# The triangular inverse of the delta-rule layer spread over two tile steps

## The chip, the cores and the metric

The kernel runs on one core of one Trainium2 chip, as one launch. The metric is the device time of that launch in microseconds (us); lower is better. The engines are PE (TensorE, matmuls; its weight loads are shown as PEld), DVE (VectorE), ACT (ScalarE), POOL (GpSimd) and SP (SyncE, which issues the DMAs here). Each engine works through its own list of instructions in order, and waits on semaphores for the others.

## What is computed

One layer of an encoder with two mixers. The change touches one stage of it, the chunked gated delta rule (DeltaNet): 4 heads of 128, 1024 prompt tokens with a state that starts at zero, and 64 sample tokens with a given state.

```python
def chunk_gated_delta(q, k, v, g, beta, s0):
    ...
    A = jnp.where(strict, jnp.einsum('bhnid,bhnjd->bhnij', k_beta, k) * dmask, 0.0)
    eye = jnp.eye(C, dtype=F32)
    T = lax.linalg.triangular_solve(eye + A, jnp.broadcast_to(eye, A.shape),
                                    left_side=True, lower=True)
    u = T @ v_beta
    w = T @ (k_beta * jnp.exp(decay)[..., None])
    qk = jnp.einsum('bhnid,bhnjd->bhnij', q, k) * dmask
    ...
    def step(S, inp):
        u_n, w_n, qk_n, qd_n, kd_n, gl_n = inp
        v_new = u_n - w_n @ S
        o_n = qd_n @ S + qk_n @ v_new
        S = S * gl_n[..., None, None] + jnp.einsum('bhck,bhcv->bhkv', kd_n, v_new)
        return S, o_n
```

## The kernel before

The whole layer is one hand-ordered program: for every engine there is a function that writes its instructions in the order in which they run, and semaphores (`g_X`, `g_Pb` and so on) hold the engines together. Before the delta-rule stage come the input projection, the S5 mixer and a gated unit (GLU); behind it come the output projection (`wo_pe`) and the feed-forward part, in which PE is busy nearly all the time.

The stage works on `TILES` = 9 tiles of 128 tokens: 8 of the prompt (`PTILES`) and one with the 64 sample tokens. One tile step `t` does the following for the four heads.

- **Preparation of a tile** (called n): `turn_kq` transposes k and q on PE, ACT sums their squares (`squares_k`, `squares_q`), POOL makes scales of them (`scales`), `gram` gives k times k, `coupling` on DVE makes A of it, `turn_A` transposes A, ACT copies it out (`keep_A`), and DVE builds the first blocks of the inverse and the masked levels of A (`first_blocks`, `first_level`, `later_levels`). `turn_v` transposes v into the bank in which k stood, once ACT has taken k from it (`k_decayed`); `scores`, `causal` and `q_decayed` prepare q's part.
- **The inverse**: blocks double in six levels. In a level PE makes P from X and the level's part of A (`level`, first half, L1128; 8 matmuls of 64x64), ACT copies P out of PSUM (`keep_P`, L1282), PE makes two products of P and X (L1137, L1139; 16 matmuls), DVE adds them to X (`grow_X`, L1507). Each next level needs that sum. Level 5 (L1125, L1133) is half as large. An f32 matmul leaves two records in the trace, so the counts there are twice these. The sample tile has five levels.
- **The state** (`state`): k times the state S (L1150), DVE makes the right sides (`right_sides`, L1514), new values V (L1154), ACT copies them (`keep_V`, L1302), then per head two matmuls of the output and one of the new state (L1161 to L1163), and DVE updates S (`new_state`, L1522).
- **The output** of tile t - 1 is scaled (POOL `out_scale`, DVE `out_rows`), transposed (`turn_o`, L1192) and written (`mix`), and two pieces of unrelated work stand in every step: `ada_rows` (L1170) and `ada_columns` (L1186), with `mod_rows` and `mod_columns` on DVE.

The order is that of the code: in step t PE runs levels 0 to 5 of tile t, and between them the preparation of tile t + 1. A level on PE waits for ACT (`g_Pb`) and DVE (`g_X`) per head; each head has a PSUM bank of its own for all levels. Banks 4 to 7 are for outputs, k and v, q and scores, and A. Two sets of most buffers alternate. In the last step ACT and DVE also split the first output weights into two parts (`wo_high`, L1695, and `wo_low`, L1699), with `tile_hi` and `tile_lo` for the first tiles of the mix. `wo_pe` waits for the last state (`g_S`).

## Time and profile before

| | |
|---|---|
| median of 3 runs | 1418.52 us (1415.66 to 1419.41) |
| the profiled execution's own time | 1418.34 us |
| its span, first to last instruction | 1416.6 us |
| PE busy, share of the span | 1365.3 us, 96% |
| delta-rule stage, from the first matmul of an inverse to the first of the output projection | 394.92 to 592.01 us |
| mean granted TensorE clock | 0.989 |

Times inside the trace count from the start of the span. 1.7 us lie around the span. A row of the timeline gives start, length, engine, line, operation, output and inputs and a count of merged records; a bracket behind it says how long the engine was idle before and who ended that.

### The profile page before, as it was taken

What the parts mean: (1) busy time and instruction counts of PE and PEld (TensorE: products, weight loads), DVE (VectorE), ACT (ScalarE), POOL (GpSimd) and SP (SyncE); (2) the same over time, 40 slices, a digit from 0 to 9 for tenths busy, and PEclk for the clock granted to TensorE, in tenths of its full rate; (3) what the DMA queues carried; (4) which work ended last, traced back from release to release, by engine and by line L of the source; (5) the groups of instructions that cost most, each with busy time, mean ns of one, the idle gap of its engine ahead of it and who ended that gap; (6) DMA issues with size and microseconds to landing.
All of it is one profiled execution on the core that took longest, in us unless ns stands there. A gap on an engine that the chain in (4) does not pass through costs nothing.

```text
span 1416.6 us, 29230 instructions
## 1 busy us (share of the span) xinstructions
PE 1365.3 (96%) x10652; PEld 1243.7 (88%) x10652; DVE 948.4 (67%) x1593; ACT 590.8 (42%) x1455; POOL 569.3 (40%) x645
## 2 busy tenths in 40 slices
PE   6999899989989999999999999999999999999997
PEld 4899899988978888888799999999999997887675
DVE  6517786774366666788879656666666567576388
ACT  6524344345566656525544333333333325443220
POOL 4887857771033434233331443432443434000051
PEclk8999999999999999999999999999999999999999
DMA  9431435335364545432133454554444448997794
GB/s 345 124 107 42 113 101 134 104 88 152 98 217 132 164 134 166 139 124 75 67 105 105 135 175 145 163 187 159 131 152 157 149 154 331 357 373 255 266 326 173
DMA packets 184409, 234.64 MB, mean 166 GB/s; under 512 B 17708, under 2 KB 118640, under 8 KB 184304
## 3 DMA queue, kind: packets, MB, share of 16 engines
q1 hardware_dynamic: 180128, 221.36, 48.3%
q10 hardware_dynamic: 4176, 11.89, 2.1%
q8 instruction: 65, 1.06, 0.3%
q14 instruction: 40, 0.33, 0.1%
HBM read 170.29 MB, written 61.73 MB: 164 GB/s over the span
## 4 chain that ended last, share of the span: by engine, by line
PE 61%; DVE 7%; ACT 4%; issue 3%; POOL 1%; DMA 1%; SPq 0%; POOLq 0%; DVEq 0%; ACTq 0%
PE bank L2350 30%; PE bank L2264 11%; PE bank L305 3%; PE bank L1674 2%; PE bank L1128 2%; PE bank L1137 2%; PE bank L1634 2%; PE bank L2281 1%; PE bank L1139 1%; PE bank L1170 1%; ACT hp L1724 1%; PE bank L1161 1%; DVE stat L1757 1%; ACT vp L1275 1%; DVE xt L1792 1%
## 5 line engine op out<-in xcount | busy, mean ns | idle before, releaser
L2264 PE MATMUL bank<-split 128*128 128x512 f32 x924 | 212.3, 390 | 3.0 <-DVE split L2397 2.3
L2264 PEld LDWEIGHTS bank<-split 128*128 128x128 f32 x924 | 172.7, 188 | 44.8 <-DVE split L2393 5.2
L2350 PE MATMUL bank<-Tlo,rh 128*128 128x272 f32 x640 | 184.7, 289 | 0.0
L2350 PE MATMUL bank<-Thi,rh 128*128 128x272 f32 x640 | 184.2, 288 | 0.0
L2350 PE MATMUL bank<-Thi,rl 128*128 128x272 f32 x640 | 184.0, 288 | 0.0
L305 PE MATMUL bank<-hT_hi,whi 128*128 128x384 f32 (+1 forms) x504 | 166.7, 331 | 2.4 <-DVE wlo L295 2.2
L305 PE MATMUL bank<-hT_hi,wlo 128*128 128x384 f32 (+1 forms) x504 | 164.9, 327 | 0.0
L305 PE MATMUL bank<-hT_lo,whi 128*128 128x384 f32 (+1 forms) x504 | 164.8, 327 | 0.0
L2350 PE MATMUL bank<-hT_lo,rh 128*128 128x272 f32 x480 | 138.5, 289 | 0.0
L2350 PE MATMUL bank<-hT_hi,rl 128*128 128x272 f32 x480 | 138.4, 288 | 0.0
L2350 PE MATMUL bank<-hT_hi,rh 128*128 128x272 f32 x480 | 137.9, 287 | 0.0
L2350 PEld LDWEIGHTS bank<-Thi,rl 128*128 128x128 f32 x640 | 120.5, 188 | 0.0
L2350 PEld LDWEIGHTS bank<-Thi,rh 128*128 128x128 f32 x640 | 120.5, 188 | 0.0
L2350 PEld LDWEIGHTS bank<-Tlo,rh 128*128 128x128 f32 x640 | 120.4, 188 | 0.0
L1963 DVE TENSOR_TENSOR rl<-sums,rh 128x512 fp32r<-128x512 f32 x80 | 61.7, 773 | 85.6 <-ACT rh L1959 85.0
L2368 ACT ACTIVATE split<-rW 128x512 fp32r<-128x512 f32 x77 | 48.6, 631 | 138.4 <-PE bank L2264 57.5
L2393 DVE TENSOR_TENSOR split<-rW,split 128x512 fp32r<-128x512 f32 x77 | 56.6, 738 | 67.7 <-ACT split L2368 67.4
L305 PEld LDWEIGHTS bank<-hT_hi,whi 128*128 128x128 f32 x504 | 95.1, 189 | 4.0 <-DVE wlo L295 2.5
L1959 ACT ACTIVATE rh<-sums 128x512 fp32r<-128x512 f32 x80 | 49.1, 625 | 111.0 <-PE bank L2350 71.1
L305 PEld LDWEIGHTS bank<-hT_lo,whi 128*128 128x128 f32 x504 | 95.1, 189 | 0.0
L305 PEld LDWEIGHTS bank<-hT_hi,wlo 128*128 128x128 f32 x504 | 95.0, 189 | 0.0
L2350 PEld LDWEIGHTS bank<-hT_hi,rh 128*128 128x128 f32 x480 | 90.7, 189 | 0.0
(450 smaller groups left out, 3358.3 us busy)
## 6 DMA issues: line engine op xcount, KB each, us to landing
wada<-w_ada SPq DMA_DIRECT2D x12, 2048.0 KB, 9.1
raw<-w_up SPq DMA_DIRECT2D x40, 512.0 KB, 5.0
wsum<-w_down SPq DMA_DIRECT2D x11, 1024.0 KB, 5.6
wt<-wsum SPq DMA_DIRECT2D x11, 1024.0 KB, 4.0
rW<-wt SPq DMA_DIRECT2D x44, 256.0 KB, 6.6
split<-split SPq DMA_DIRECT2D x22, 512.0 KB, 5.2
wraw<-w_in SPq DMA_DIRECT2D x21, 512.0 KB, 4.4
rows<-convrow ACTq DMA_DIRECT2D x16, 577.5 KB, 3.7
```

Of the source, the lines that this page charges most:

```text
L305: last = nc.tensor.matmul(ps[banks[c]][:, 0:cw], w[:, slot, k * P:(k + 1) * P], a[:, k, c0:c0 + cw], start=(k == 0 and n == 0), stop=(k == ...
L1128: last = pe.matmul(ps[h][q, 0:HB], Lc[x][q, l, h, :], Xc[x][q, h, 0, :], start=True, stop=True)
L1137: pe.matmul(ps[h][q, P:P + HB], Xc[x][q, h, 1, :], Pb[q, h, 0:HB], start=True, stop=True)
L1139: last = pe.matmul(ps[h][q, P + HB:2 * P], Pb[q, h, 0:HB], Xc[x][q, h, 1, :], start=True, stop=True)
L1634: last = pe.matmul(ps[up_bank(1, j, c)][:, 0:cw], w[:, j, k * P:(k + 1) * P], a[:, k, c0:c0 + cw], start=(k == 0 and n == 0), stop=(k == K ...
L1674: last = pe.matmul(ps[2 * s + h][0:n, :], a[:, s, k * P:k * P + n], w[:, k, cols], start=(k == 0 and m == 0), stop=(k == KD - 1 and m == 2))
L1959: act.activation(ring_hi[slot4(m, n)], operand(i, n, m), ACT.Copy).then_inc(on["st_hi"], 1)
L1963: dve.tensor_tensor(ring_lo[slot4(m, n)], operand(i, n, m), ring_hi[slot4(m, n)].bitcast(F32), ALU.subtract).then_inc(on["st_lo"], 1)
L2264: last = pe.matmul(ps[down_bank(q, r)][:], a[:, rows], w, start=(k == 0 and m == 0), stop=(k == KH - 1 and m == 2))
L2350: last = pe.matmul(ps[banks[c]][:, 0:NC], w[:, ks], a, start=(n < 3 and k == 0 and p == 0), stop=(k == 3 and p == 2), skip_group_check=True)
L2368: act.activation(w_hi_of(s), raw_w(s), ACT.Copy).then_inc(on["d_hi"], 1)
L2393: dve.tensor_tensor(w_lo_of(s), raw_w(s), w_hi_of(s).bitcast(F32), ALU.subtract).then_inc(on["d_lo"], 1)
```

## The change

- **The inverse over two steps.** Step t now has three rounds (`round_of`). Round r does level 3 + r of tile t and level r of tile t + 1: P of the one, P of the other, then the products of the one and of the other. Before the loop stand levels 0 to 2 of tile 0 alone, with the preparation of tile 1 between them.
- **Preparation two tiles ahead** (n = t + 2, `AHEAD_OF`), all of it behind the rounds. It needs a third set of `stg`, `kdec` and `sc` and a second `Pb`; the load of q, k, v is issued for tile t + 3.
- **Pairs of heads.** Two heads share a PSUM bank for P and the products: even tiles have banks 0 and 1, odd tiles 2 and 3. ACT copies P, and DVE adds, for two heads at once (2 instructions for 4, twice as wide), and V likewise; semaphores count pairs.
- **State part split** into `read_state`, `new_values` and `outputs`, with `turn_q`, `turn_o`, `turn_v` and `ada_columns` between them; `turn_A`, `scores` and `ada_rows` follow all four heads' outputs. `read_state` waits until the next tile's level 2 has left its bank.
- **Smaller scale formulas.** q's scale isn't applied before the norm of the output any more; POOL does 9 small operations per tile where it did 12 (the two of 8 columns become 4 wide), `scales_k` waits for k's squares alone, and `causal` stands ahead of `q_decayed`, which now waits for the outputs of step t (`g_kv`), since it fills a buffer that they read.
- **End of the stage.** Four pairs of `wo_high` and `wo_low` move from the last step into the one before it. Step 7 has no preparation, and the last step has two levels left.

```diff
-        (kdec0, QK0, qd0, vp0, Pb, Rb, Vb, ob, junk, Sst, Xc0, Xf0), endD = seq(
-            WO2, ("kdec0", hp), ("QK0", hp), ("qd0", hp), ("vp0", hp), ("Pb", hp), ("Rb", hp), ("Vb", hp), ("ob", hp),
+        (kdec2, QK0, qd0, vp0, vp1, Pb0, Rb, Vb, ob, junk, Sst, Xc0, Xf0), endD = seq(
+            WO2, ("kdec2", hp), ("QK0", hp), ("qd0", hp), ("vp0", hp), ("vp1", hp), ("Pb0", hp), ("Rb", hp), ("Vb", hp), ("ob", hp),
...
+        stg, Pb = (stg0, stg1, stg2), (Pb0, Pb1)
+        Lc, kdec, QK, qd, vp, Xc, Xf = (Lc0, Lc1), (kdec0, kdec1, kdec2), (QK0, QK1), (qd0, qd1), (vp0, vp1), (Xc0, Xc1), (Xf0, Xf1)
...
-        lv = lambda t, l, h: (t * LV + l) * HEADS + h
+        PAIRS = HEADS // 2
...
+        ROUNDS = LV // 2
+        AHEAD_OF = 2
...
+                    sp.wait_ge(on["g_E"], (t + 2) * 3 + 3)
+                    decay_rows(t + 4)
+                if t + 3 < TILES:
+                    sp.wait_ge(on["g_kS"], (t + 1) * HEADS)
+                    sp.wait_ge(on["g_qd"], t + 1)
+                    qkv(t + 3)
                 if 1 <= t and t + 1 < TILES:
...
-                for h in range(HEADS):
+                if l in (0, ROUNDS):
+                    pe.wait_ge(on["g_S"], count(t if l else t - 1) * HEADS)
+                for p in range(PAIRS):
...
+            def level_X(t, l):
+
+                x = t % 2
+                for p in range(PAIRS):
+                    pe.wait_ge(on["g_Pb"], lvp(t, l, p) + 1)
+                    for i, h in enumerate((2 * p, 2 * p + 1)):
+                        if l == LV - 1:
...
+            def round_of(t, r):
+
+                units = [(u, l) for u, l in ((t, ROUNDS + r), (t + 1, r)) if 0 <= u < TILES and l <= top(u)]
+                for u, l in units:
+                    level_P(u, l)
+                for u, l in units:
+                    level_X(u, l)
+
+            def read_state(t):
+                if t + 1 < TILES:
+                    pe.wait_ge(on["g_X"], lvp(t + 1, ROUNDS - 1, PAIRS - 1) + 1)
...
-                    pe.matmul(hb(h, 0), stg[:, x, k_ + h, :], Sst[:, st, h, :], start=True, stop=True).then_inc(on["g_kS"], 1)
+                    if t:
+                        pe.wait_ge(on["g_S"], (t - 1) * HEADS + h + 1)
+                    pe.matmul(kS_of(h), stg[t % 3][:, k_ + h, :], Sst[:, state_of(t), h, :], start=True, stop=True).then_inc(on["g_kS"], 1)
+
+            def new_values(t):
                 pe.wait_ge(on["g_Xf"], since("g_Xf", t + 1))
+                pe.wait_ge(on["g_R"], t * HEADS + HEADS)
                 for h in range(HEADS):
-                    pe.wait_ge(on["g_R"], t * HEADS + h + 1)
-                    pe.matmul(hb(h, 3), Xf[x][:, h, :], Rb[:, h, :], start=True, stop=True).then_inc(on["g_V"], 1)
+                    pe.wait_ge(on["g_X"], lvp(t, top(t), h // 2) + 1)
...
+            def outputs(t, heads):
+                x, st = t % 2, state_of(t)
                 pe.wait_ge(on["g_qd"], t + 1)
                 pe.wait_ge(on["g_QK"], t + 1)
...
+            level_P(0, 0)
+            turn_k(1)
+            level_X(0, 0)
+            level_P(0, 1)
+            gram(1, 0)
+            gram(1, 1)
+            level_X(0, 1)
+            level_P(0, 2)
+            turn_q(1, ALL)
+            level_X(0, 2)
+            turn_v(1, ALL)
+            turn_A(1)
+            scores(1)
             for t in range(TILES):
-                n, more = t + 1, t + 1 < TILES
-                level(t, 0)
+                n = t + AHEAD_OF
+                more = n < TILES
+                for r in range(ROUNDS):
+                    round_of(t, r)
                 if more:
-                    turn_kq(n)
-                level(t, 1)
-                level(t, 2)
+                    turn_k(n)
+                    gram(n, 0)
+                    gram(n, 1)
+                read_state(t)
+                if more:
+                    turn_q(n, ALL)
                 if t:
                     turn_o(t - 1)
-                level(t, 3)
                 if more:
-                    scores(n)
-                level(t, 4)
-                if more:
-                    gram(n)
+                    turn_v(n, ALL)
+                new_values(t)
                 if t:
                     ada_columns(t - 1)
+                outputs(t, ALL)
                 if more:
-                    level(t, 5)
                     turn_A(n)
-                    turn_v(n)
-                state(t)
+                    scores(n)
                 if t < PTILES:
                     ada_rows(t)
...
             def keep_P(t, l):
                 rows = DOWN if l == LV - 1 else slice(0, P)
-                for h in range(HEADS):
-                    act.wait_ge(on["g_P"], lv(t, l, h) + 1)
-                    act.activation(Pb[rows, h, 0:HB], ps[h][rows, 0:HB], ACT.Copy).then_inc(on["g_Pb"], 1)
+                for p in range(PAIRS):
+                    act.wait_ge(on["g_P"], lvp(t, l, p) + 1)
+                    act.activation(Pb[t % 2][rows, pair(p), 0:HB], bank_of(t, p)[rows, 0:P].rearrange("p (h c) -> p h c", c=HB),
+                                   ACT.Copy).then_inc(on["g_Pb"], 1)
 
...
-                n, more = t + 1, t + 1 < TILES
-                if more:
-                    keep_P(t, 0)
-                    keep_P(t, 1)
-                    squares_k(n)
-                    keep_P(t, 2)
-                    squares_q(n)
+                n = t + AHEAD_OF
+                more = n < TILES
+                if t < PTILES:
                     keep_P(t, 3)
-                    decay(n)
+                    keep_P(t + 1, 0)
+                    if more:
+                        decay_diff(n, FIRST2)
                     keep_P(t, 4)
-                    decay_exp(n)
-                    k_decayed(n)
+                    keep_P(t + 1, 1)
+                    if more:
+                        decay_diff(n, LAST2)
                     keep_P(t, 5)
+                    keep_P(t + 1, 2)
                     whole_X(t)
-                    keep_A(n)
-                    v_scaled(n)
+                    if more:
+                        decay_exp(n)
+                        decay_row(n)
+                        squares_k(n)
+                        k_decayed(n)
+                        squares_q(n)
                     keep_V(t)
+                    if more:
+                        v_scaled(n)
+                        keep_A(n)
+                    else:
+                        act.wait_ge(on["g_X0"], 2 * TILES)
+                        act.wait_ge(on["g_QK"], TILES)
+                        act.wait_ge(on["g_qd"], TILES)
+                        wo_high(act, 0)
+                        wo_high(act, 1)
                     squares_o(t)
+                    if not more:
+                        wo_high(act, 2)
...
             def q_decayed(n):
+                pool.wait_ge(on["g_E"], n * 3 + 3)
+                pool.wait_ge(on["g_kv"], count(n - 1) * HEADS)
+                pool.tensor_tensor(qd[n % 2][:], stg[n % 3][:, q_:q_ + HEADS, :], erow[:], ALU.mult).then_inc(on["g_qd"], 1)
+
...
-                if t:
-                    out_scale(t - 1)
-                if t + 1 < TILES:
-                    scales(t + 1)
-                    q_decayed(t + 1)
-                    causal(t + 1)
-            out_scale(TILES - 1)
+                n = t + AHEAD_OF
+                if n < TILES:
+                    scales_k(n)
+                    scales_q(n)
+                    causal(n)
+                    q_decayed(n)
...
+                    if l == LV - 1:
...
-                        dve.tensor_copy(Xf[x][UP, h, DOWN], ps[h][UP, P + HB:2 * P]).then_inc(on["g_X"], 1)
...
-                n, more = t + 1, t + 1 < TILES
+                n = t + AHEAD_OF
+                more, nxt = n < TILES, t + 1 < TILES
                 if t:
                     mod_rows(t - 1)
-                grow_X(t, 0)
-                if not more:
-                    wo_low(dve, 0)
-                grow_X(t, 1)
+                for r in range(ROUNDS):
+                    if ROUNDS + r <= top(t):
+                        grow_X(t, ROUNDS + r)
+                    if nxt:
+                        grow_X(t + 1, r)
+                        if r == 0:
+                            keep_scores(t + 1)
                 if t:
                     out_rows(t - 1)
-                if not more:
...
-                    wo_low(dve, 2)
-                grow_X(t, 3)
+                right_sides(t)
...
-                if not more:
-                    wo_low(dve, 3)
-                grow_X(t, 4)
...
                     coupling(n)
-                if more:
-                    grow_X(t, 5)
...
+                elif nxt:
+                    wo_low(dve, 0)
+                    wo_low(dve, 1)
                 else:
+                    wo_low(dve, 4)
                     tile_lo(dve, 0, 0)
                 new_state(t)
                 if more:
-                    keep_scores(n)
+                    first_level(n)
```

PE in step 1 before: level 0, and the transposes of the next tile behind it (Xc is X, Lc the level's part of A).

```order
L1128 MATMUL bank<-Xc_136,Lc_138 64x64 x8
L1137 MATMUL bank<-Pb,Xc_136 64x64 x2
L1139 MATMUL bank<-Xc_136,Pb 64x64 x2
L1137 MATMUL bank<-Pb,Xc_136 64x64 x2
L1139 MATMUL bank<-Xc_136,Pb 64x64 x2
L1137 MATMUL bank<-Pb,Xc_136 64x64 x2
L1139 MATMUL bank<-Xc_136,Pb 64x64 x2
L1137 MATMUL bank<-Pb,Xc_136 64x64 x2
L1139 MATMUL bank<-Xc_136,Pb 64x64 x2
L1078 MATMUL bank<-ident,stg 128x128 x4
L1082 MATMUL bank<-ident,stg 128x128 x4
```

PE in step 0 after, from the start of the first round.

```order
L1161 MATMUL bank<-Xc_153,Lc_119 64x64 x8
L1161 MATMUL bank<-Xc_139,Lc_141 64x64 x8
L1175 MATMUL bank<-Pb_147,Xc_153 64x64 x2
L1177 MATMUL bank<-Xc_153,Pb_147 64x64 x2
L1175 MATMUL bank<-Pb_147,Xc_153 64x64 x2
L1177 MATMUL bank<-Xc_153,Pb_147 64x64 x2
L1175 MATMUL bank<-Pb_147,Xc_153 64x64 x2
L1177 MATMUL bank<-Xc_153,Pb_147 64x64 x2
L1175 MATMUL bank<-Pb_147,Xc_153 64x64 x2
L1177 MATMUL bank<-Xc_153,Pb_147 64x64 x2
L1175 MATMUL bank<-Pb_156,Xc_139 64x64 x2
```

Where one P was followed by its own products, P of a second tile stands between them, and after four heads' products (8 rows) come the other tile's instead of transposes.

PE before, from the gram matrix to the first head's outputs.

```order
L1186 MATMUL bank<-sel,modrow_123 128x2 x4
L1125 MATMUL bank<-Xc_136,Lc_138 64x64 x4
L1133 MATMUL bank<-Xc_136,Pb 64x64 x4
L1101 MATMUL bank<-ident,Am 128x128 x4
L1107 MATMUL bank<-ident,stg 128x128 x4
L1150 MATMUL bank<-Sst,stg 128x128 x4
L1154 MATMUL bank<-Rb,Xf_137 128x128 x4
L1161 MATMUL bank<-Sst,qd_134 128x128
L1162 MATMUL bank<-Vb,QK_133 128x128
L1163 MATMUL bank<-Vb,kdec_132 128x128
```

PE after, from the end of the rounds to the outputs.

```order
L1104 MATMUL bank<-ident,stg_155 128x128 x4
L1125 MATMUL bank<-stg_155 128x128 x4
L1199 MATMUL bank<-Sst,stg_116 128x128 x4
L1110 MATMUL bank<-ident,stg_155 128x128 x4
L1138 MATMUL bank<-ident,stg_155 128x128 x4
L1206 MATMUL bank<-Rb,Xf_154 128x128 x4
L1216 MATMUL bank<-Sst,qd_144 128x128
L1217 MATMUL bank<-Vb,QK_143 128x128
L1218 MATMUL bank<-Vb,kdec_133 128x128
L1216 MATMUL bank<-Sst,qd_144 128x128
L1217 MATMUL bank<-Vb,QK_143 128x128
```

The level between them is gone, `turn_A` has left the stretch, and k, gram, q and v of a tile two ahead stand around the read of the state.

POOL at the start of the stage, before.

```order
L1383 TENSOR_TENSOR sc<-sc 128x4
L1393 TENSOR_TENSOR EB<-E,triu 128x512
L1388 TENSOR_TENSOR qd_142<-stg,erow 128x512
L1410 MEMSET Sst 128x512
L1413 MEMSET Xf_151 64x4x64
L1413 MEMSET Xf_137 64x4x64
L1377 TENSOR_SCALAR sc<-sc 128x8
```

POOL there after; the rows after the gap are those of tile 1.

```order
L1489 TENSOR_SCALAR sc<-sc 128x4
L1499 TENSOR_TENSOR EB<-E,triu 128x512
L1494 TENSOR_TENSOR qd_144<-stg_116,erow 128x512
L1513 MEMSET Sst 128x512
L1516 MEMSET Xf_154 64x4x64
L1516 MEMSET Xf_140 64x4x64
...
L1489 TENSOR_SCALAR sc<-sc 128x4
L1499 TENSOR_TENSOR EB<-E,triu 128x512
L1494 TENSOR_TENSOR qd_138<-stg_117,erow 128x512
```

Ahead of EB now stands q's one operation; EB comes ahead of qd for the later tiles as well, and tile 1 has its EB and qd before the loop.

## Rows read from the trace of the kernel before

**Rows 1.** The page, part 1: busy time, share of the span and instructions.

```profile
PE 1365.3 (96%) x10652; PEld 1243.7 (88%) x10652; DVE 948.4 (67%) x1593; ACT 590.8 (42%) x1455; POOL 569.3 (40%) x645
```

**Rows 2.** Busy time by stretch: steps 1, 2 and 8; us, then each engine, clock, DMA.

```profile
417.10:439.50 22.40, 22.19 (x360) 18.95 (x356) 14.91 (x49) 13.88 (x71) 7.92 (x15) 1.00 0.50 154
439.50:462.10 22.60, 22.39 (x360) 19.01 (x356) 14.96 (x49) 13.92 (x71) 8.00 (x15) 1.00 0.49 153
...
575.00:592.00 17.00, 15.27 (x281) 13.97 (x278) 15.93 (x42) 13.11 (x39) 3.12 (x5) 1.00 0.41 141
```

**Rows 3.** Timeline of step 2, PE, with the start of step 3.

```profile
439.56 0.68 PE L1128 MATMUL bank<-Xc,Lc 64*64 64x64 f32 x16
...
440.21 0.33 PE L1137 MATMUL bank<-Pb,Xc 64*64 64x64 f32 x4
...
441.29 0.66 PE L1078 MATMUL bank<-ident,stg 128*128 128x128 f32 x4
...
442.31 0.68 PE L1128 MATMUL bank<-Xc,Lc 64*64 64x64 f32 x16
...
442.97 0.33 PE L1137 MATMUL bank<-Pb,Xc 64*64 64x64 f32 x4
...
443.95 1.01 PE L1128 MATMUL bank<-Xc,Lc 64*64 64x64 f32 x16
...
452.85 0.67 PE L1125 MATMUL bank<-Xc,Lc 64*64 64x64 f32 x8
...
453.48 0.67 PE L1133 MATMUL bank<-Xc,Pb 64*64 64x64 f32 x8
...
457.42 0.46 PE L1161 MATMUL bank<-Sst,qd 128*128 128x128 f32 x2 [0.21 <-ACT Vb L1302]
...
460.26 1.92 PE L1170 MATMUL bank<-wada,csil4b 128*32 128x512 f32 x16
...
462.12 0.68 PE L1128 MATMUL bank<-Xc,Lc 64*64 64x64 f32 x16
```

**Rows 4.** Timeline of step 2, DVE and ACT.

```profile
440.70 0.99 DVE L1507 TENSOR_TENSOR Xc<-Xc,bank 128x128 f32<-128x128 f32 x4 [0.21 <-PE bank L1139]
...
450.08 0.62 ACT L1262 ACTIVATE E<-E 128x512 f32<-128x512 f32 x1
...
450.61 1.14 ACT L1267 ACTIVATE kdec<-bank,gcol 128x128 f32<-128x128 f32 x4
...
452.26 1.12 DVE L1457 SCALAR_TENSOR_TENSOR Am<-bank,sc,E 128x128 f32<-128x128 f32 x4 [0.89 <-PE bank L1095]
...
453.80 0.84 ACT L1296 ACTIVATE Xf<-Xc 64x256 f32<-64x256 f32 x2
...
454.78 0.77 ACT L1289 ACTIVATE ATc<-bank 64x256 f32<-64x256 f32 x2
...
455.54 1.13 DVE L1514 SCALAR_TENSOR_TENSOR Rb<-bank,sc,vp 128x128 f32<-128x128 f32 x4 [1.08 <-PE bank L1150]
```

**Rows 5.** Groups by line, 395 to 592 us: busy us, mean ns | idle before.

```profile
L1240 ACT ACTIVATE junk<-bank 128x128 f32<-128x128 f32 x32 | 8.4, 284 | 0.0
```

**Rows 6.** Timeline where the stage starts, PE, DVE and POOL.

```profile
391.33 1.90 DVE L1465 TENSOR_TENSOR Xc<-Am,mask1c 64x256 f32<-64x256 f32 x2
...
391.25 1.27 POOL L1388 TENSOR_TENSOR qd<-stg,erow 128x512 f32<-128x512 f32 x1
...
394.92 1.12 PE L1128 MATMUL bank<-Xc,Lc 64*64 64x64 f32 x16 [2.42 <-DVE Lc L1473]
```

**Rows 7.** The instructions of L1465: duration ns min/median/max, first and last start.

```profile
L1465 DVE TENSOR_TENSOR Xc<-Am,mask1c x18: 402/422/1465, 391.3 to 570.0; 64x256 f32<-64x256 f32 x18
```

**Rows 8.** PE's busy time, granted clock and DMA in two stretches there.

```profile
391.00:394.40 3.40, 1.06 (x8) 0.99 1.04 399
394.40:397.80 3.40, 2.88 (x49) 0.50 1.05 386
```

**Rows 9.** Timeline, the first matmul of the output projection.

```profile
592.01 0.47 PE L1674 MATMUL bank<-wo_hi,whi 128*128 128x512 f32 x1 [0.54 <-DVE Sst L1522]
```

More of the change, by code:

```diff
@@ L1029, in gdn_loads @@
             sp.dma_start(Sst[:, 1, :, :], I["state_gdn"].rearrange("h k v -> k h v")).then_inc(on["s_state"], 16)
+            for t in range(2, 4):
+                sp.wait_ge(on["g_E"], (t - 2) * 3 + 3)
+                decay_rows(t)
             for t in range(TILES):
@@ L1102, in turn_A, with turn_v, level_P @@
                 last.then_inc(on["g_AT"], 1)
-            def turn_v(n):
+            def turn_v(n, heads):
                 pe.wait_ge(on["g_kdec"], n + 1)
-                for h in range(HEADS):
-                    last = pe.transpose(h4(5)[:, h, :], stg[:, n % 2, v_ + h, :], ident[:])
-                last.then_inc(on["g_T"], 1)
-            def level(t, l):
+                for h in heads:
+                    last = pe.transpose(h4(5)[:, h, :], stg[n % 3][:, v_ + h, :], ident[:])
+                if HEADS - 1 in heads:
+                    last.then_inc(on["g_T"], 1)
+            def level_P(t, l):
                 x = t % 2
                 if l == LV - 1:
-                    pe.wait_ge(on["g_AC"], since("g_AC", t + 1))
+                    pe.wait_ge(on["g_AC"], since("g_AC", t * 2 + 2))
                 else:
@@ L1187, in ada_columns, with turn_o @@
                 last.then_inc(on["mod_T"], 1)
-            def turn_o(t):
+            def turn_o(t, heads=ALL):
                 pe.wait_ge(on["g_ob"], t + 1)
-                for h in range(HEADS):
+                for h in heads:
                     last = pe.transpose(h4(4)[:, h, :], ob[:, h, :], ident[:])
-                last.then_inc(on["g_oT"], 1)
+                if HEADS - 1 in heads:
+                    last.then_inc(on["g_oT"], 1)
             glu_last(pe, 0)
@@ L1253, in decay @@
                 act.wait_ge(on["g_EB"], n)
-                for h in range(HEADS):
+                for h in heads:
                     last = act.activation(E[:, h, :], drow[:, n % 2, h, :], ACT.Abs, scale=-1.0, bias=col(DEC, n, h))
-                last.then_inc(on["g_E"], 1)
-                act.wait_ge(on["g_qd"], n)
-                act.activation(f4(erow[:]), f4(drow[:, n % 2, :, :]), ACT.Exp).then_inc(on["g_E"], 1)
+                if HEADS - 1 in heads:
+                    last.then_inc(on["g_E"], 1)
             def decay_exp(n):
```

282 lines of the change are left out of this document (155 added, 127 removed).

## The prediction, made before the changed kernel ran

> **What bounds the kernel now.** The page's first part comes first: PE is busy 96% of the span [rows 1], so only PE's time counts, and a gain must come out of gaps between its instructions. Then the busy time by stretch. A step of the delta-rule stage takes 22.6 us, DVE works 15.0 of it, ACT 13.9 and POOL 8.0 [rows 2]: none of them is the bound. PE's own column reads 22.4, but matmul ends are modelled; the column beside it, its weight loads, is the honest one, and it is busy 19.0 us. The missing 3.5 us or so per step are what the change can reach. Third, the timeline of step 2 says where they lie. A level starts at 439.56 and its products at 440.21; in the level that starts at 443.95 the eight matmuls of P are stretched, since each head waits for DVE's sum [rows 3]. I read two costs out of the rows:
>
> - P without a wait takes about 0.52 us (estimated from the 0.65 us to the products in level 0, less a gap of about 0.14 in which ACT copies the first head). The products take 0.93: 442.97 to the next P at 443.95 is 0.98, with 0.05 of start-up [rows 3]. So a level's issue is 1.45 us. Level 5 takes 0.5 and 0.5 (452.85, 453.48, and a similar stretch behind it).
> - Each turn from 64x64 matmuls to 128x128 and back costs about 0.1 to 0.2 us: the products end near 441.14 and the transposes start at 441.29, and the same is lost at 442.31 [rows 3].
>
> The gaps of step 2, about: five copies of P waited for, 1.0; one P stretched by the sums, 0.3; four round trips between shapes inside the levels, 1.0; right sides and V waited for ahead of the outputs (up to 457.42, where the row names ACT's copy), 0.7; and 0.5 around `ada_rows` (460.26 to the next level at 462.12 is 1.86, of which 1.4 is issue) [rows 3]. Sum 3.5, as in rows 2.
>
> **The rounds.** Two P in a row, then two sets of products: 2 x (0.52 + 0.93) = 2.9 us. For the third round 0.52 + 0.52 + 0.52 + 0.93 = 2.5, so 8.3 us in all. Do the waits hide? A row of DVE's sum starts 0.25 us behind the last matmul it needs, four heads take 0.99 [rows 4]; I take 0.42 for a pair (the DVE operations of 256 columns take 0.42 [rows 7]). From the round's start the products of the first tile's second pair are issued by 1.95, their sum is there by 2.65, and the next round's P wants it at 2.9 + 0.25. For the second tile: issued by 2.9, sum by 3.6, wanted at 2.9 + 0.52 + 0.25 = 3.67. It just fits. ACT's copies have 0.5 us of other matmuls over them. I put the wait at nothing; if that cover is short by 0.2 us, it costs 0.2 x 26 rounds = 5 us.
>
> **Behind the rounds**, times from their end, E. PE has k (0.45), gram (0.9), the read of the state (0.9), q and o (0.9), v (0.45), new values (0.9), columns (0.8), outputs (2.7), A (0.45), scores (0.9), `ada_rows` (1.4 and 0.45 behind it). With 0.25 for the changes of shape that is 11.45 if nothing waits. What may wait:
>
> - `turn_v` wants kdec. ACT in order: the X copy 0.84 (begun at E - 0.9, since the last copy of P is early), exponential 0.62, row 0.61, squares 1.1 (four at 0.284 [rows 5]), kdec 1.14 [rows 4]: done at E + 3.4, wanted at 3.3. Costs 0.15.
> - `new_values` wants the right sides: the state is read by 2.4, +0.3, +1.13 [rows 4] = 3.85, wanted at 3.9. Nothing.
> - V's copy of the second pair is done at 5.55, but PE has the columns until 5.65. Nothing.
> - The outputs now stand right behind `ada_columns`, and wait until DVE has taken these out of bank 4 (`mod_cols`). Before, level 5 and the state covered this. Last column matmul 5.6, +0.25, DVE 0.15, +0.05: outputs start at 6.05, not 5.65. Costs 0.4, 7 times.
> - The POOL work of a tile moves too: `q_decayed` waits for the outputs (9.05) and takes 1.27 [rows 6]. It touches DVE's `first_level`, which waits for `turn_A` (9.2), ACT's copy 0.77 [rows 4], so 10.25. Three operations of 0.42 make 11.6. The second tile's level 0 wants that at 12.1 + 0.5 = 12.6. Slack 1.0, nothing.
>
> The sum is 11.45 + 0.15 + 0.4, and 0.05 for rounding: 12.05. A full step takes 8.3 + 12.05 = 20.4 us against 22.6. DMA: q, k, v are loaded a step ahead of need as before, and the queue is busy 0.5 [rows 2]: hidden.
>
> **The fill.** Before, the first level starts at 394.92 [rows 6]. After, POOL's two big operations come about 0.7 us earlier there, so L1465, which took 1.90 us for two instructions beside POOL's qd [rows 6] where the median of one is 0.422 [rows 7], should go free: first level at 394.0. Then levels 0 to 2 of tile 0 stand alone, each at about 2.5 us, for PE waits for ACT and DVE and fills in with tile 1's transposes. ACT has differences, exponential, squares, kdec and squares in line, so kdec of tile 1 is ready at 402.9, DVE's sum at 403.4, `coupling` (1.12 [rows 4]) at 404.5. Now POOL has EB and qd of tile 1 to do, 404.2 to 406.8, and `first_blocks` (1.25) and `first_level` (1.27) wait for it: 409.3. The first round's second P starts there; the round counts as begun at 408.9.
>
> The row of L1465 shows the mechanism: an instruction with both inputs in SBUF that began in POOL's 1.27 us lasted 1.465 [rows 6, 7]. By the Trainium skill (SBUF — State Buffer, "SBUF: two separate sides") DVE with two SBUF inputs and a GpSimd operation that reads SBUF exclude each other, and whichever starts first holds the ports for the whole instruction. The trace agrees. By that rule DVE could also slip in between EB and qd, which would give 1.3 us back.
>
> In the gaps the clock may fall. Before, PE worked 1.06 of 3.4 us, and in the 3.4 us that followed the granted clock was 0.50, 1.2 instead of 2.4 GHz [rows 8]; the level there took 0.88 instead of 0.65 to its products [rows 3, 6]. After, PE has nothing from about 406.5 to 409.3. I add 1.4 us for one such stretch (a round of 2.9 at half speed in 3.4 us loses at most 1.7; the bound below is 0). First round: 410.3.
>
> **The sum.** Step 0 (no outputs to turn, no columns; kdec and then V's copy let the outputs start at 5.1, so that `ada_rows` ends at 11.15): 8.3 + 11.15 = 19.45, to 429.8. Steps 1 to 6: 6 x 20.4 = 122.4, to 552.2. Step 7 has no preparation: the state is read after DVE's last sum (0.75), outputs end at 7.9, `ada_rows` until 9.85: 18.15, to 570.3. Step 8: ACT takes P only behind four `wo_high` (11.4 after E of step 7), DVE behind four `wo_low`; level 4 starts at 13.95, the state is read at 15.95, right sides at 18.2, outputs 20.35 to 23.05, and the last state stands at 24.1 behind `wo_low` and `tile_lo`: 14.55 us against 17.0 before [rows 2], to 584.9. The output projection started at 592.01 [rows 9]. The stage ends 7.1 us earlier, and behind it PE is the bound, so all of it arrives. 1418.34 - 7.1 = 1411.2; the profiled execution is 0.2 under the median of 1418.52. I say **1411 us**.
>
> **Rivals.**
>
> - *A better fill* (0.17). DVE gets between POOL's two (1.3), the clock holds (1.4), the columns don't hold up the outputs (0.4 x 7 = 2.8). For: all three are placed at the end of what the rows bear. Against: nothing removes the `mod_cols` wait. All of it gives 1405.7, two of three about 1408.
> - *The rounds don't hide* (0.22). The second tile's sum has 0.07 us to spare. If a pair's sum takes 0.6, or ACT's two half-widths are slow, 0.2 to 0.3 us go in each of 26 rounds: 1416 to 1419. Against it: DVE and ACT are free then.
> - *ACT becomes the bound* (0.09), slower than before. ACT's chain from the last P to kdec is 4.3 us long in one line and PE has 4.2 us over it. It decides from there: each 0.1 us later is a 0.1 us later v, new values, copy of V and outputs in 8 steps. If the copy of X and the two exponentials don't start until k's transposes are done or each squares step takes the 0.5 us per head that its two records add up to, ACT is 1.5 us late: 12 us, 1423.
> - *The step doesn't overlap at all*: pairs give only fewer waits. Then the fill costs 13 us for nothing. The order of PE shows otherwise, 0.02.
>
> **How the numbers follow.** Forecast 0.50: 1408.5 to 1414. Faster by more than 0.3% (4.3 us, about what a measurement of this kernel can tell from no change) is under 1414.3: forecast, better fill and a little of the second rival, 0.70. Within 0.3% (1414.3 to 1422.8): most of the second rival, 0.20. Slower: 0.10. The range of 8 in 10 goes from 1405.5, the better fill in full, to 1418, most of the second rival.
>
> **What would show it.** In the trace of after: steps 20.4 us apart, PE's weight loads still busy 19.0 of them; rounds of 2.9, 2.9 and 2.5; PE idle about 0.4 us ahead of the outputs, released by DVE's modc; the second tile's first P of the stage near 409, with POOL's EB and qd over DVE's L1573 (was L1465); a low clock within a few us of it; first matmul of the output projection near 585. Rounds above 3.1 mean the second rival; an idle time ahead of `turn_v` or the outputs that ACT releases, of over 1 us, the third. The forecast is wrong if the fill ends later than 413, or if a step takes over 21.3 us.

## The result, and the profile after

| | before | after |
|---|---|---|
| median of 9 runs each | 1418.5 us (1415.66 to 1420.39) | 1424.2 us (1418.99 to 1428.6) |
| the profiled execution's own time | 1418.34 us | 1418.99 us |
| its span | 1416.6 us | 1417.3 us |
| first matmul of the output projection | 592.01 us | 592.75 us |
| mean granted TensorE clock of it | 0.989 | 0.985 |

The ratio is 1.0044, 95% interval 1.0029 to 1.0059: the kernel became slower, where 1411 us was forecast. The profiled execution of after is the fastest of its nine; its median lies 5.2 us above it.

The page, part 1, answers [rows 1]. The same 10652 matmuls are busy 15 us less, their weight loads 8 us less, and the span is no shorter: what the change took out of busy time came back as idle time of PE.

```profile
PE 1350.2 (95%) x10652; PEld 1235.4 (87%) x10652; DVE 945.5 (67%) x1487; ACT 584.0 (41%) x1331; POOL 548.8 (39%) x618
```

Busy time by stretch (as [rows 2]): two stretches of 22 us over steps 1 and 2 (about half a us more than a step), step 5, step 8.

```profile
428.00:450.00 22.00, 20.37 (x368) 17.92 (x363) 14.74 (x38) 13.65 (x63) 6.82 (x11) 1.00 0.50 158
450.00:472.00 22.00, 20.22 (x364) 17.77 (x356) 14.72 (x38) 13.65 (x60) 6.82 (x11) 1.00 0.52 158
514.30:534.40 20.10, 19.55 (x357) 17.58 (x356) 14.58 (x36) 13.19 (x57) 7.38 (x12) 1.00 0.52 159
578.30:592.70 14.40, 9.77 (x137) 8.68 (x133) 10.31 (x22) 8.48 (x21) 1.05 (x2) 1.00 0.51 166
```

The weight loads, which are the honest column, are busy 17.9, 17.8 and 17.6 us (19.0 a step was forecast), so steps 1 and 2 hold hardly more work than step 5 and are 1.4 and 1.5 us longer all the same. By the first matmul of `ada_rows` (L1225) steps 1 to 7 take 21.50, 21.65, 22.26, 21.44, 20.14, 22.39 and 19.66 us. Step 5 is the step that was forecast (20.4); the others hold something that it doesn't. The waits of PE from the end of step 0 to the end of step 6 name it (columns: who waited, for whom, us in total, times, longest):

```profile
PE bank L1177 <- issue: 3.4, 2, 1.9
PE bank L1216 <- DVE modc L1543: 3.3, 6, 0.7
PE bank L1175 <- issue: 1.3, 1, 1.3
PE bank L1161 <- issue: 1.2, 1, 1.2
PE bank L1125 <- issue: 0.9, 1, 0.9
PE bank L1161 <- DVE Xc L1615: 0.2, 1, 0.2
```

"issue" is time in which PE waits for nothing that the profile shows: no semaphore, no engine. In the timeline one such stretch stands in the middle of the four matmuls that P takes for a pair of heads, which have their waits at their head and none between them:

```profile
434.97 0.45 PE L1158 MATMUL bank<-Xc,Lc 64*64 64x64 f32 x5
435.28 0.33 PE L1161 MATMUL bank<-Xc,Lc 64*64 64x64 f32 x4
436.79 0.39 PE L1161 MATMUL bank<-Xc,Lc 64*64 64x64 f32 x6 [1.17 <-issue]
```

From the last record of PE before such a stretch to the next one there are 1.39, 1.49, 1.76, 1.19, 2.07 and 1.57 us, before 436.79, 459.15, 481.70, 504.72, 543.68 and 566.24. Counted through PE's records (weight loads, matmuls, and its few others), the instructions that end the stretches are numbers 6310, 7078, 7846, 8614, 9894 and 10662, all 166 above a multiple of 256. A step has 726 such records in nearly all cases, so the place in the code changes and the count does not. The kernel before has one such stretch, 0.65 us, before number 8870, which is 166 above a multiple of 256 too:

```profile
516.75 0.60 PE L1088 MATMUL bank<-stg 128*128 128x128 f32 x3 [0.38 <-issue]
```

The DMA view holds the other half. Each packet of the queue named "instruction" that PE waits for carries 16 KB. The first fence is 431.6 to 434.2, the second 434.2 to 435.4, just ahead of the stretch above (queue, kind: packets, MB, share of 16 engines).

```profile
q1 hardware_dynamic: 506, 1.04, 104.2%
```

```profile
q1 hardware_dynamic: 226, 0.46, 100.0%
q8 instruction: 1, 0.02, 5.2%
```

PE enters the 256 instructions that begin with number 6054 (block 6054 from here on) at 431.56. The packet starts 2.74 us later, while data packets keep the DMA engines full, ends at 435.30, and PE goes on at 436.79. Those data are one transfer of 2 MB, the next modulation weights (`wada`, issued at 429.41 when `ada_rows` has freed the buffer), in flight from 430.5 to 437.8, over the rounds. All six stretches end 1.3 to 1.5 us behind the end of such a packet. Step 5 has the same transfer and no stretch: there PE enters its block at 517.12 and the packet starts at 517.40, when the first data packets have just started (517.31), so it comes ahead of most of them.

The timeline at the fill, rows of POOL, then DVE, then PE: POOL's two operations lie over `first_blocks` (L1573) as forecast, and the second tile's P begins at 409.21 (forecast 409.3).

```profile
404.56 1.27 POOL L1499 TENSOR_TENSOR EB<-E,triu 128x512 f32<-128x512 f32 x1
405.79 1.45 POOL L1494 TENSOR_TENSOR qd<-stg,erow 128x512 f32<-128x512 f32 x1
...
405.02 2.50 DVE L1573 TENSOR_TENSOR Xc<-Am,mask1c 64x256 f32<-64x256 f32 x2
...
409.21 1.08 PE L1161 MATMUL bank<-Xc,Lc 64*64 64x64 f32 x16 [2.01 <-DVE Lc L1581]
```

### The profile page after: what moved, and what is told of

It reads as the page before. It is cut to its first block, busy times and chain, and to the rows that moved or that the text cites. A ratio compares the mean times of both kernels' runs of the same rounds, so it can differ in the third digit from the quotient of the medians.

```text
span 1417.3 us, 28855 instructions
## 1 busy us (share of the span) xinstructions
PE 1350.2 (95%) x10652; PEld 1235.4 (87%) x10652; DVE 945.5 (67%) x1487; ACT 584.0 (41%) x1331; POOL 548.8 (39%) x618
## 4 chain that ended last, share of the span: by engine, by line
PE 61%; DVE 6%; ACT 3%; issue 3%; DMA 2%; POOL 1%; SPq 1%; POOLq 0%; ACTq 0%; DVEq 0%
PE bank L2459 28%; PE bank L2373 12%; PE bank L308 4%; PE bank L1783 2%; PE bank L1743 2%; PE bank L1161 2%; PE bank L1177 1%; PE bank L2390 1%; PE bank L1175 1%; ACT hp L1833 1%; PE bank L1225 1%; PE bank L1216 1%; PE bank L1206 1%; PE bank L1217 1%; PE bank L1218 1%
```

## Experiments

Theory: PE's instructions come in blocks of 256, one 16 KB packet each; the next block is asked for when one is entered; the dense rounds use a block up in 3.8 us, and beside the 2 MB load the block takes 5.2 us and more to come. Rivals: the idle stretches are waits for other engines that the profile doesn't see, the loss is the clock alone, or rounds simply don't run as densely as PE's queue allows.

**The changed kernel once more** (`rerun`, no edit).

> The changed kernel as it is, once more. Theory (PE waits for its own instructions): one idle stretch of 1.1 to 2.1 us with no releaser per step, in six or so of the nine steps, at PE instruction numbers that differ by multiples of 256 from those of the first trace (6310, 7078, 7846, 8614, 9894, 10662), so at the same matmuls again; output projection begins between 591 and 595. Rival (the stretches are chance, such as DMA traffic or a late semaphore): they stand at other matmuls or in other number. If low clock stretches inside the stage are what makes the median 5 us longer than the profiled run, this trace shows more than the two seen before, or the mean clock falls with the time over the runs.

Measured: 1424.18 us (1419.67 to 1430.91), ratio to the kernel before (here and below) 1.0035 (1.0020 to 1.0049). Its profiled execution is a long one (span 1429.2 us) and shows where a good part of the spread of times comes from: the output projection starts at 601.1 in it, not 592.75, and outside the 591 to 595 expected. The stretches stand at the same instructions (0.65 to 2.62 us), and there are four periods of low clock in steps 1 to 8 (3.4 to 6.8 us each, 20.5 us together, at most half of it lost), where the first trace has none in the stage behind 412.7. The fourth, 6.8 us from 588.9, lies in step 8 and behind no such stretch. Windows ahead of the other three, and then these three periods:

```profile
455.80:459.20 3.40, 1.85 (x53) 1.65 (x50) 1.13 (x4) 2.88 (x8) 0.00 (x0) 1.00 0.51 186
479.70:483.10 3.40, 1.69 (x48) 1.48 (x46) 1.18 (x4) 2.83 (x8) 0.00 (x0) 1.00 0.38 136
544.50:547.90 3.40, 1.29 (x45) 1.15 (x39) 1.26 (x3) 0.62 (x3) 0.00 (x0) 1.00 0.89 332
...
459.20:462.60 3.40, 3.40 (x35) 3.28 (x32) 1.44 (x3) 1.04 (x9) 0.00 (x0) 0.50 0.24 80
483.10:489.90 6.80, 6.43 (x36) 6.31 (x37) 1.95 (x6) 2.46 (x14) 1.87 (x5) 0.50 0.12 41
547.90:551.30 3.40, 3.10 (x63) 2.96 (x65) 0.99 (x3) 1.76 (x6) 0.00 (x0) 0.50 0.05 18
```

Ahead of each fall PE had worked 1.3 to 1.9 of 3.4 us, since an idle stretch of 1.55 to 2.40 us lay in it. The same pattern, in the kernel before, is [rows 8]. So in this execution the stretches seem to cost twice: once themselves, once by the clock behind them. Three of its six have no such period behind them.

**Twenty transposes more ahead of the stage** (`shift`): 40 records of PE more, and the same work behind them.

```diff
+            pe.wait_ge(on["g_kdec"], 1)
+            for _ in range(5):
+                for h in range(HEADS):
+                    pe.transpose(h4(5)[:, h, :], stg[0][:, v_ + h, :], ident[:])
             turn_v(0, ALL)
             level_P(0, 0)
```

> The changed kernel with 20 more transposes (40 more PE instructions) ahead of the loop, where PE is idle in the fill; their result is overwritten by the same values. Theory (blocks of 256 instructions): the idle stretches keep their instruction number modulo 256 (166 when counted from the start), so each lies 40 instructions, 20 matmuls, earlier in the work of its step than in the changed kernel. Rival (the stretches belong to an operation of the rounds): they stay at the same matmuls, and their instruction numbers move by 40.

Measured: 1424.06 us, span 1422.3. The stretches stand before numbers 6310, 7078, 7846, 8614 and 10662 again (1.96, 1.83, 1.71, 2.03, 2.09 us), now 40 records earlier in the work; the sixth is not before 9894 but, with 0.54 us, before 9382, which is 166 above a multiple of 256 too:

```profile
435.20 0.27 PE L1175 MATMUL bank<-Pb,Xc 64*64 64x64 f32 x2 [1.74 <-issue]
...
459.18 0.39 PE L1161 MATMUL bank<-Xc,Lc 64*64 64x64 f32 x6 [1.61 <-issue]
```

They go by the count of instructions, not by what these do. That rules out a hidden wait for another engine. (This is a single execution, with four periods of low clock in steps 1 to 4; its time is not compared.)

**Preparation spread between the rounds** (`spread`): `turn_k` behind round 0, both `gram` behind round 1.

```diff
-                if more:
-                    turn_k(n)
-                    gram(n, 0)
-                    gram(n, 1)
+                    if more and r == 0:
+                        turn_k(n)
+                    if more and r == 1:
+                        gram(n, 0)
+                        gram(n, 1)
```

> One part changed: k's transposes stand behind round 0 and the gram matrix behind round 1, instead of both behind round 2. PE's work is the same, with two more changes of shape per step (about +0.5 us). Theory (instructions arrive too slowly for three dense rounds in a row): the idle stretches of 1.1 to 2.1 us shrink or vanish, steps of 20.5 to 20.9 us on average instead of 21.5, output projection at 585 to 589, 4 to 7 us ahead of the changed kernel. Rival (the stretches come from a wait for ACT or DVE between the rounds): the stretches stay, and steps get longer by the 0.5 us, output projection at about 596.

Measured: 1426.82 us, ratio 1.0058 (1.0040 to 1.0077), output projection from 597.45: the number of the rival, not the 585 to 589 of the theory. The stretches of the first steps are indeed shorter (0.20, 0.88 and 0.76 us, and none in step 4), the last two are 1.74 and 1.56. But what stood behind the rounds had been the cover of ACT's and DVE's chains, and those waits now lie open, in every step:

```profile
PE bank L1199 <- DVE Xc L1616: 3.7, 7, 0.5
PE bank L1138 <- ACT kdec L1344: 3.0, 5, 0.8
PE bank L1216 <- DVE modc L1544: 2.9, 6, 0.6
```

**The same, with `scores` ahead of the outputs** (`spread_scores`).

```diff
                 if t:
                     ada_columns(t - 1)
+                if more:
+                    scores(n)
                 outputs(t, ALL)
                 if more:
                     turn_A(n)
-                    scores(n)
```

> As spread, and q's and k's scores stand between the columns and the outputs. Theory: they fill the 0.4 to 0.7 us in which PE waits for DVE's modc ahead of the outputs, so a step gets another 0.3 to 0.5 us shorter, 3 us over the stage, unless turn_A, ACT's copy and DVE's first level, 0.9 us later now, reach the next round: the slack there was 1.0 us. Rival: that chain is the next bound, and the step stays as in spread, with PE idle ahead of the second tile's level 0.

Measured: 1427.01 us, ratio 1.0058 (1.0041 to 1.0075). The wait for `modc` goes, from eight times to two at the stage's end, but the longer ones of PE's own stretches are back (0.72, 1.55, 0.48, 0.34, 2.14, 1.62 and 2.25 us). The 0.6 us a step that the cover gave did not reach the end; what fits is a block that came no sooner for it.

**The chains follow too** (`even`): `gram` in two halves, the earlier output's turn behind round 1, ACT's squares and kdec within the rounds.

```diff
+                    if more and r == 0:
+                        turn_k(n)
+                        gram(n, 0)
+                    if more and r == 1:
+                        gram(n, 1)
+                        if t:
+                            turn_o(t - 1)
...
```

> The preparation of the tile two ahead is spread over the step again, as far as the other engines can follow: k's turn and the first pair of k times k behind round 0, the second pair and the turn of the earlier output behind round 1; ACT's order follows (k's squares in round 1, the decayed k in round 2), and DVE scales the earlier output rows in round 0. Theory 1 (dense rounds outrun the fetch of PE's instructions): with other work between the rounds PE's own idle stretches shrink to 0.5 to 1.0 us, and without the wait ahead of v that the first such spread had (0.83 to 1.07 us a step) the steps are 20.6 to 21.2 us, the output projection starts at 587 to 592, and the time is 1416 to 1420, about that of the kernel before. Theory 2 (what is lost is the clock alone, or waits for other engines): the idle stretches stay, and steps of 21.5 to 22.5 us give 1423 to 1427.

Measured: 1428.71 us, ratio 1.0068 (1.0052 to 1.0085). A miss (1416 to 1420 was expected). In steps 1 to 6 PE's own stretches shrink, to 0.6, 1.0, 0.15 and 1.2 us, and the wait for kdec is gone, as meant; the one before 10662, beside the output weights, is 2.40. But each step keeps three waits of about 0.5 us (the read of the state for DVE's last sum, V, and the columns), and steps 1 to 5 take 21.9 to 22.5 us, steps 6 and 7, with periods of low clock in them, 24.8 and 22.8. Spreading pays for the fetch with cover.

**P and products of one tile, then of the other** (`serial`).

```diff
                 for u, l in units:
                     level_P(u, l)
-                for u, l in units:
                     level_X(u, l)
```

> In each round P and the products of one tile stand together, then those of the other; nothing else moves. Theory 1 (PE runs out of fetched instructions in the dense rounds): the six waits for ACT's copy of P that the alternation had hidden come back, some 0.15 to 0.3 us each, 1.0 to 1.5 us a step, but a slower round leaves the fetch more time, so PE's own idle stretches (1.2 to 2.1 us, six of them) shrink by about as much; the steps stay at 21.5 to 22.0 us and the output projection starts between 592 and 597. Theory 2 (the idle stretches have nothing to do with how dense the rounds are): they stay as long, and every step is longer by the 1.0 to 1.5 us; the output projection starts at 600 or later, and the time is about 1431.

Measured: 1428.14 us, ratio 1.0060 (1.0045 to 1.0075), output projection from 601.91. Each theory is half right: the stretches shrink, to 0.9, 0.7, 1.6, 0.9 and 0.8 us, as theory 1 says, but the output projection starts where theory 2 put it; the returned waits for ACT's copies are larger than my 0.15 to 0.3 (0.36 us each from one matmul to the next, six a step), so steps 1 to 6 take 22.1 to 23.35, and 6.8 us of low clock lie in step 8. By itself this run doesn't decide.

**An eighth of the modulation weights** (`small_ada`). From tile 2 on one slice of eight is loaded; the modulation columns are not computed from the right weights.

```diff
-                sp.dma_start(wada2[:, t % 2, :, :], wad[:, :, c * ADA_N:(c + 1) * ADA_N]).then_inc(on["ada"][t % 2], 16)
+                ks = KD if t < 2 else 1
+                sp.dma_start(wada2[:, t % 2, 0:ks, :], wad[:, 0:ks, c * ADA_N:(c + 1) * ADA_N]).then_inc(on["ada"][t % 2], 16)
```

> From tile step 2 on the load of the modulation weights brings one of its eight slices (the modulation columns are not computed from the right weights any more), so that some 7/8 of the large transfers of this stage are gone; every instruction of every engine stays where it is. Theory 1a (a block of PE instructions takes 5.3 to 5.9 us to come because its packet shares the DMA engines with these transfers): the idle stretches of PE of its own fall from 1.2 to 2.1 us to below 0.5, the steps go to 20.1 to 20.5 us, the output projection starts at 583 to 587. Theory 1b (the turnaround of a block is the same on quiet DMA engines): the stretches stay at 1.2 to 2.1 us at the same instruction numbers, and the output projection starts at 591 to 600, as in the runs of the changed kernel.

Measured: 1413.95 us, ratio 0.9964 (0.9948 to 0.9980). Every instruction of PE stands where it did, and steps 1 to 6 take 20.1 to 20.5 us. PE's waits up to 550 us (the one stretch of its own that is left there, 0.37 us before number 9126, is too short to be listed):

```profile
PE bank L1217 <- DVE modc L1544: 3.0, 6, 0.6
```

The stretch before number 10662 is still there, 2.39 us. It is the control within the run: there the first 2 MB of output weights are in flight (552 to 557.9):

```profile
q1 hardware_dynamic: 504, 1.94, 80.7%
q8 instruction: 1, 0.02, 1.1%
```

**The whole load, at another place** (`late_ada`).

```diff
-                if t + 2 < PTILES:
-                    sp.wait_ge(on["ada_mm"], ADA0 + t + 1)
-                    ada(t + 2)
+                if 1 <= t and t + 1 < PTILES:
+                    sp.wait_ge(on["ada_mm"], ADA0 + t)
+                    sp.wait_ge(on["g_kS"], (t + 1) * HEADS)
+                    ada(t + 1)
```

> The 2 MB load of the modulation weights for tile t + 1 is issued in the middle of step t, behind k times the state and behind the loads of q, k, v and z, and no longer at the end of step t - 1; nothing else is changed, and the kernel computes everything. Theory 1 (these transfers, in flight just while the dense rounds run, delay the packets that bring PE's instructions): PE's own idle stretches in steps 1 to 6 fall from 1.2 to 2.1 us to below 0.5, except the one at instruction 10662 (step 7), beside which the load of the first output weights runs; the steps are 20.1 to 20.6 us, the output projection starts at 583 to 587, up to 4 later with periods of low clock in the stage, and the time is 1410 to 1415. Theory 2 (the run with an eighth of the load gained by its smaller total traffic): the stretches come back with the full load, wherever it lies; the output projection starts at 590 or later and the time is 1420 to 1425.

Measured: **1412.23 us** (1410.67 to 1415.36), ratio 0.9954 (0.9938 to 0.9969). Steps 1 to 6 take 20.13 to 20.43 us. The same bytes are moved, 12 us later in the step. PE's waits from 427 to 548, and the DMA queues from 431.2 to 432.4, when the block's packet has the engines to itself:

```profile
PE bank L1217 <- DVE modc L1544: 2.9, 6, 0.6
```

```profile
q8 instruction: 1, 0.02, 5.3%
```

PE enters block 6054 at 431.05 here, the packet starts 0.2 us later (2.74 in the trace of after), and the next block is entered at 434.89 with no gap. Only the stretch before 10662 (1.56 us), beside the output weights, remains. The output projection starts at 585.45 us, where the prediction had put it (584.9), and the span is 1410.1: against the kernel before 6.6 us off the stage, 6.5 off the span.

**The same edit on the kernel before** (`before_late`; the diff is the one above).

> The kernel before with the same edit of the load's place alone. It has one idle stretch of PE's own in the stage, 0.65 us, since its blocks of 256 instructions take 4.9 us and more. Expected under both theories: at most that 0.65 us goes, 1417 to 1419, within 0.1% of the kernel before; if it gained 5 us or more, the load's place would be worth that with or without the change, and the fetch of instructions would not be what ties it to the dense rounds.

Measured: 1418.88 us, ratio 0.9999 (0.9991 to 1.0008). Its one stretch (0.65 us) is gone, and the median does not move. The load's place is worth nothing unless PE is dense enough.

**Two more covers** (`late_all`): besides, `scores` ahead of the outputs, and the first load of output weights in two halves, the second in the middle of step 7.

```diff
...
                 if t == PTILES - 2:
                     sp.wait_ge(on["ada_mm"], ADA0 + t + 1)
-                    wo_load(0)
+                    wo_load(0, (0,))
+                if t == PTILES - 1:
+                    sp.wait_ge(on["g_kS"], (t + 1) * HEADS)
+                    wo_load(0, (1,))
...
```

> As the run with the later load, and two more edits: the scores stand between the modulation columns and the outputs (covers the 0.7 to 0.9 us in which PE waits there for the columns' addition), and the first load of the output weights is halved, one half at its place, the other behind k times the state of step 7. Theory 1: steps of 19.5 to 20.0 us, the idle stretch at instruction 10662 shorter by half, the output projection starts at 579 to 584, and the time is 1406 to 1411. Rival: the scores only move the wait elsewhere (behind them PE waits for V's copy or the causal product), steps as in the run with the later load and the time within 1 us of it.

Measured: **1409.98 us** (1404.08 to 1412.48), ratio 0.9926 (0.9906 to 0.9945). Steps 1 to 6 take 19.54 to 19.74 us, the stretch before 10662 is down to 0.86, output projection from 581.52. With PE's instructions at hand, the scores do cover the wait for the columns (0.6 us a step), which they could not in the spread kernel. This one beats both kernels, and so does the run with the load moved alone.

## Why the prediction was wrong

Its ledger against the trace of after, in us:

| term | forecast | measured | difference |
|---|---|---|---|
| step 1 starts | 429.8 | 429.3 | -0.5 |
| steps 1 to 6 | 122.4 | 129.4 | +7.0 |
| step 7 | 18.15 | 19.66 | +1.5 |
| step 8 | 14.55 | 14.4 | -0.15 |
| output projection starts | 584.9 | 592.75 | +7.85 |

- **The failed step is "11.45 if nothing waits", and 8.3 us for three rounds beside it.** Both are issue times, and their sum is right as such: step 5 took 20.14 in all, and so did five of the steps 1 to 6 once the load was moved (`late_ada`, where the rounds take 7.9 us from the first P to k's transposes). What they left out is that PE's instructions are themselves a load. "DMA: q, k, v are loaded a step ahead of need [...] hidden" looked at the queue's busy share (0.5) and its data alone. Three rounds are 520 records that start within 7.75 us (`late_ada`), 3.8 us for a block of 256. In the kernel before the packet comes as late beside the same 2 MB transfer (3.36 and 3.43 us behind the entry of blocks 7078 and 8614), but in steps 1 to 6 a block lasts 4.9 us and more, and the transfer costs one stretch of 0.65 us. Five stretches, 7.9 us from record to record, make up nearly all of the 8.5 us by which steps 1 to 6 exceed six times 20.14; the sixth is step 7's +1.5. Against its own sign of being wrong, a step of over 21.3 us, these six average 21.56. That moving the load removes the five, and that the kernel before gains nothing by it, is shown.
- **Clock.** The sum has one low period, 1.4 us, near 409; the trace has it (409.3 to 412.7, 0.50), though what it cost there was not measured apart. The forecast was set against the profiled execution, and the median of after is 5.2 us above that. In `rerun` and in `shift` the low periods of steps 1 to 7 (0.50, 1.2 instead of 2.4 GHz) begin at PE's own idle stretches; `late_ada` has none of either between 412.6 and step 7, and its median is 1.6 us above its fastest run. That the stretches bring the low clock on is what these rows suggest; no run held the one and varied the other, and they are not all of it: the six runs of `late_all`, whose one stretch is 0.86 us, still lie between 1404.08 and 1412.48 us, the fastest at a mean clock of 0.99, four of the others at 0.981 or 0.982.
- **Fill**: right, to 0.1 us in the start of the second tile's P (409.21 against 409.3), by the mechanism named: DVE's two operations of L1573 took 2.50 us beside POOL's.
- **`mod_cols`**: right in place, small in size: 0.4 was put, 0.5 to 0.7 measured, and `late_all` gives back 0.6 a step by covering it. Other waits (kdec, right sides, V) are hidden as argued, or cost less than was allowed: a clean step took 20.14 us against 20.4 (the terms add up to 20.35, and rounding that up put 0.3 us into the six steps).
- **"So all of it arrives"**: right. Moved loads take 6.6 off the stage and 6.5 off the span [rows 9 for before].
- **Rivals.** Nothing of the better fill came: DVE did not get between POOL's two, the clock fell and the columns held the outputs up. "The rounds don't hide" did not happen in the form written: the wait for DVE's sum in the rounds is 0.2 us in all of six steps. ACT did not become the bound. The slower side had a mechanism that I did not list: that a denser PE meets the fetch of its own program.
- **A page that bore on it.** The Trainium skill (Runtime: NRT & Kernel Launch, Instruction fetch mechanics) says that instructions are refilled in 16 KiB blocks of 256 by a DMA queue of the sequencer's own while the current ones run, mostly hidden. The trace agrees on the block and on the queue; "hidden" holds for the kernel before but for 0.65 us, and fails here. The Trainium skill (DMA: Bandwidth & Descriptors, Queues, rings and completion order) says that an engine takes turns between its queues packet by packet. The 2.74 us against 0.2 us until the packet starts show that it waits while data are in flight. Taking turns with single packets of the profile would not last that long: they are of 2 KB and took about 0.08 us each (an estimate from 506 packets on 16 engines in 2.6 us). What the packet waits for in the 2.7 us stays open. Read together with the 2 MB transfer in the trace of before, the two would still have made this a rival.

## What to carry to other kernels

When a change packs small matmuls closer, divide PE's instructions by the time: in the six cases of after, blocks of 256 that PE alone would have used up in 3.8 to 4.7 us were followed by waits of 1.2 to 2.1 us for the program beside a large load, blocks of 4.8 to 5.4 us (`spread`, `even`, `serial`, the kernel before) by at most 1.0. An idle stretch that the profile gives to "issue", at a fixed distance in PE's count, is its mark; move the large transfer to where PE's instructions are long, before pulling work apart. Work put between dense parts can cost more in uncovered waits of other engines than it saves.

## What the runs showed of the hardware

- In the rounds a block of 256 PE instructions came as one 16 KB packet, most of them taking 0.9 to 1.3 us. With the DMA engines quiet (`late_ada`, blocks used up in 3.7 to 4.0 us) it started 0.2 to 0.8 us after the block before it was entered; beside a 2 MB load, ahead of the six stretches of after, 2.7 to 3.4 us after, and PE went on 1.3 to 1.5 us behind its end. That makes, as an estimate from these, 2.4 to 3.6 us from one block's start to the next one being there, against 5.2 to 5.9 us as measured beside the load. The blocks of the first case showed no gap.
- In the rounds only the next block was waited for, and no trace shows PE with several blocks in hand there. Where PE is slower the packets do not start at a block's entry: in the trace of after some start 9 us and more behind it, and between 865 and 1131 us none is recorded at all while PE runs through 17 blocks. Why is open.
- Idle stretches of 1.7 to 2.6 us inside dense work were followed by periods of 3.4 or 6.8 us at 0.50 of the clock in `rerun` and `shift` (seven of ten such), and the one of 2.4 us in `small_ada` and in `even` too; none of the six of after (1.2 to 2.1 us) and none of those in `spread_scores` (1.5 to 2.25 us) was.
